# Opening of a two-block network: ten of sixteen modulation tiles made by TensorE as rows and turned, six left to VectorE

## The reference

```
mod_lat = silu(c) @ w_mod[0] + b_mod[0]        # 6 pieces of 1024: shift, scale, ...
mod_ctx = silu(c_ctx) @ w_mod[0] + b_mod[0]
u_ctx = h_ctx * (1 + mod_ctx[1]) + mod_ctx[0]  # 256 tokens
u_lat = h_lat * (1 + mod_lat[1]) + mod_lat[0]  # 512 tokens
lat = u @ mla_w_in                             # 1024 -> 512 + 256 + 64, then RMS norms
```

## Time and profile before

| | us |
|---|---|
| median of 3 runs (lowest, highest) | 4194.78 (4189.4, 4211.54) |
| the profiled execution, its own time | 4194.11 |
| its span, first to last instruction | 4192.3 |
| first matmul of the opening | 17.3 |
| first matmul behind the opening's barrier | 112.7 |
| mean granted TensorE clock | 0.967 of full speed |

### The profile page before, as it was taken

One profiled execution on the slowest core, in us unless ns is written; L12 is line 12 of the kernel. 1 busy time (PEld: TensorE's weight loads), 2 busy tenths in 40 slices (PEclk: granted clock), 3 DMA queues, 4 the chain that ended last, 5 costly groups with the idle time before them and its releaser, 6 DMA issues. The chain is left out here.

```text
span 4192.3 us, 53471 instructions
## 1 busy us (share of the span) xinstructions
PE 3870.7 (92%) x19878; PEld 2820.9 (67%) x19878; DVE 2551.6 (61%) x4594; ACT 1205.3 (29%) x2519; POOL 1304.3 (31%) x1515
## 2 busy tenths in 40 slices
PE   8899999999999797888999999989999989669998
PEld 4577555555555586777888886568755566668887
DVE  7634899652488884557688876645534428923354
ACT  3155310101222484652121112128611221341112
POOL 1175399200000068820000094849000111530001
PEclk9999999999999899999999999999999999879999
DMA  4542366331111076544345554523011375882222
GB/s 171 196 112 90 122 179 186 116 112 62 58 70 50 21 226 164 118 98 163 129 154 177 173 165 127 154 61 114 19 53 63 124 257 191 246 237 93 76 86 76
DMA packets 287968, 533.16 MB, mean 127 GB/s; under 512 B 177024, under 2 KB 184064, under 8 KB 263424
## 3 DMA queue, kind: packets, MB, share of 16 engines
q1 hardware_dynamic: 216736, 344.70, 25.5%
q0 software_dynamic: 53312, 180.00, 14.3%
q10 hardware_dynamic: 17696, 5.56, 0.6%
HBM read 430.01 MB, written 100.01 MB: 126 GB/s over the span
## 5 line engine op out<-in xcount | busy, mean ns | idle before, releaser
L570 PE MATMUL P<-hu,ring 128*128 128x384 f32 (+1 forms) x2448 | 743.0, 457 | 6.0 <-PEq L849 3.6
L570 PEld LDWEIGHTS P<-hu,ring 128*128 128x128 f32 x2448 | 465.5, 190 | 258.7 <-issue 5.8
L887 PE MATMUL P<-area,ring 128*128 128x256 f32 (+1 forms) x1880 | 484.4, 413 | 29.5 <-PEq L2605 16.0
L887 PEld LDWEIGHTS P<-area,ring 128*128 128x128 f32 x1880 | 356.1, 191 | 147.8 <-issue 38.4
L570 PE MATMUL P<-area,ring 128*128 128x256 f32 (+1 forms) x1584 | 443.2, 432 | 3.7 <-DVE area L733 3.0
L570 PEld LDWEIGHTS P<-area,ring 128*128 128x128 f32 x1584 | 301.7, 191 | 127.9 <-issue 5.4
L887 PE MATMUL P<-area,hu 128*128 128x256 f32 (+1 forms) x1104 | 297.2, 424 | 5.5 <-DVE hu L1010 5.5
L1147 POOL TENSOR_TENSOR fold<-mod,vec 128x16 f32<-128x16 f32 (+1 forms) x5 | 10.1, 2018 | 862.6 <-DMA s_fb<-area 365.0
L887 PEld LDWEIGHTS P<-area,hu 128*128 128x128 f32 x1104 | 209.3, 190 | 84.2 <-DVE hu L1010 7.7
L3010 DVE SCALAR_TENSOR_TENSOR area<-area 128x1024 f32<-128x1024 f32 x124 | 189.6, 1529 | 17.4 <-ACT area L3086 15.3
L2478 POOL TENSOR_TENSOR area<-area 128x512 f32<-128x512 f32 (+2 forms) x98 | 177.1, 1807 | 7.7
(11 more groups left out here) (495 smaller groups left out, 7193.4 us busy)
## 6 DMA issues: line engine op xcount, KB each, us to landing
ring<-in_w_ffn_in SPq DMA_DIRECT2D x44, 1024.0 KB, 4.8
area<-in_w_mod SPq DMA_DIRECT2D x70, 512.0 KB, 3.5
ring<-s_c POOLq DMA_DIRECT2D x18, 1152.0 KB, 9.4
stat<-in_w_mod SPq DMA_DIRECT2D x40, 512.0 KB, 3.4
s_c<-area POOLq DMA_DIRECT2D x32, 576.0 KB, 3.2
ring<-in_w_ffn_out SPq DMA_DIRECT2D x24, 704.0 KB, 4.1
area<-s_b POOLq DMA_DIRECT2D x16, 1024.0 KB, 6.0
hu<-s_c POOLq DMA_DIRECT2D x14, 1152.0 KB, 9.7
```

The source lines that it names most:

```text
L570: last = mm(to, col(a, k), b[:, k, :], start=fresh and k == 0, stop=k == q - 1, skip_group_check=True)
L887: last = mm(to, a[:, 128 * k:128 * k + 128], b[k], start=fresh and k == 0, stop=k == q - 1, skip_group_check=True)
```

## The change

Ten of the sixteen modulation tiles (0 to 7, 14 and 15) go from DVE to PE. Their weights are stored in another layout, two tiles together, so that PE can make a row of 256 outputs for both conditions: eight matmuls with a stationary operand of 128 x 2 (`silu_of[:, k, :]`, the silu of c and c_ctx as two columns) and 256 moving columns of weights, added up in two partitions of PSUM (`mod_row`). ACT copies the row to SBUF (`keep_row`), PE turns it back into columns with two matmuls of two moving columns (`turn_row`), and DVE adds the bias straight from PSUM. Five such pairs stand ahead of and between the products. The six tiles 8 to 13 stay on DVE.

The loads move: `conds` from the head of SP's queue to the head of POOL's, the first four projection weights as halves of 256 KB, those for k < 4 early on SP (`w_lo`), those for k >= 4 later on POOL (`w_hi`), `s5_lam` from SP to ACT. DVE makes six steps of the S5 tables between modulation tiles 1 and 2 and three more ahead of the last additions. The tails (256 tokens) of two output tiles share a PSUM bank, which frees one for the row; the copies of tiles 0 and 2 out of PSUM wait for the tile behind them, and tiles 1 and 3 are copied in two pieces.

```diff
+MOD_BY_PE = ((0, 8), (14, 16))
...
+    silu_of = c.view(25616, KD, 2)
+    row_kept = [c.view(24832 + 256 * n, 256)[0:2] for n in range(2)]
+    row = c.P[0:2, 1, 512:768]
+    pairs_of = [0, 2, 4, 6, 14]
...
-            sp.dma_start(flat(conds), ins["conds"][0:1, :].broadcast_to([128, 2 * D])).then_inc(conds_in, 16)
-            sp.dma_start(first_w[0], ins["w_mod"][0]).then_inc(mod_in[0], 16)
...
+            for k in range(0, KD, 2):
+                for n in (k, k + 1):
+                    sp.dma_start(first_w[n], ins["w_mod"][n]).then_inc(mod_in[n], 16)
                 sp.dma_start(h[:, k, 0:LAT], x[:, k, :]).then_inc(x_in[k], 16)
-            sp.dma_start(flat(raw), ins["s5_lam"]).then_inc(lam_in, 16)
+                if k == 0:
+                    for n in range(4):
+                        sp.dma_start(weights[n][:, 0:512], ins["w_mla_in"][n, :, 0:512]).then_inc(w_lo, 16)
+                sp.dma_start(h[:, k + 1, 0:LAT], x[:, k + 1, :]).then_inc(x_in[k + 1], 16)
...
+            pool.dma_start(flat(conds), ins["conds"][0:1, :].broadcast_to([128, 2 * D])).then_inc(conds_in, 16)
...
+            def mod_row(i):
+                n = pairs_of[i]
+                pe.wait_ge(mod_in[n], 16)
+                pe.wait_ge(mod_in[n + 1], 16)
+                if i == 0:
+                    pe.wait_ge(silu_v, 1)
+                else:
+                    pe.wait_ge(rows_kept, i)
+                for k in range(KD):
+                    last = mmul(row, silu_of[:, k, :], first_w[n + k // 4][:, 256 * (k % 4):256 * (k % 4) + 256],
+                                start=k == 0, stop=k == KD - 1, skip_group_check=True)
+                last.then_inc(rows_made, 1)
+            def turn_row(i):
+                if i == 0:
+                    pe.wait_ge(ident_in, 16)
+                pe.wait_ge(rows_kept, i + 1)
+                for e in range(2):
+                    last = mmul(turned_mod(pairs_of[i] + e), row_kept[i % 2][:, 128 * e:128 * e + 128], c.ident[0:2, 0:2],
+                                start=True, stop=True, skip_group_check=True)
+                last.then_inc(mods_turned, 1)
+            def product(k, between=()):
                 pe.wait_ge(shifted, k + 1)
+                if k == 0:
+                    pe.wait_ge(w_lo, 64)
+                if k == 4:
+                    pe.wait_ge(w_hi, 64)
                 for j in range(4):
-                    for a, b in BOTH:
-                        last = mmul(c.P[:, j, a:b], weights[j][:, 128 * k:128 * k + 128], u[:, k, a:b], start=k == 0, stop=k == KD - 1)
+                    w = weights[j][:, 128 * k:128 * k + 128]
+                    mmul(body(j), w, u[:, k, 0:512], start=k == 0, stop=k == KD - 1)
+                    last = mmul(tail(j), w, u[:, k, 512:T], start=k == 0 and j % 2 == 0, stop=k == KD - 1, skip_group_check=True)
                     if k == KD - 1:
                         last.then_inc(mm, 1)
+                    if j == 1:
+                        for i in between:
+                            turn_row(i)
+            mod_row(0)
+            turn_row(0)
+            product(0)
+            mod_row(1)
+            product(1, (1,))
+            product(2)
+            mod_row(2)
+            product(3, (2,))
+            product(4)
+            mod_row(3)
+            mod_row(4)
+            product(5, (3, 4))
+            product(6)
+            product(7)
...
+            act_fn(silu_of.rearrange("p k e -> p e k"), c.vec[:, at:at + 16].rearrange("p (e k) -> p e k", e=2), ACT.Silu).then_inc(silu_v, 1)
...
+            keep_row(0)
...
+            shift(0)
+            shift(1)
+            keep_row(1)
+            shift(2)
+            shift(3)
+            keep_row(2)
+            shift(4)
+            shift(5)
+            keep_row(3)
+            keep_row(4)
+            shift(6)
+            shift(7)
...
+            def scales(k):
+                dve.wait_ge(mod_in[8 + k], 16)
+                for cc in range(2):
+                    if k or cc:
+                        dve.wait_ge(made, 2 * k + cc)
+                    mod_product(c, 8 + k, cc, first_w[8 + k], junk).then_inc(made, 1)
+            def add(n, x):
+                return V.tensor_tensor(c.mod[:, n, 0:2], x, base[:, n:n + 1].broadcast_to([128, 2]), ALU.add)
+            def tile(k):
+                scales(k)
+                if k == 0:
+                    dve.wait_ge(based, 3)
+                dve.wait_ge(mods_turned, k // 2 + 1)
+                add(k, turned_mod(k))
+                dve.wait_ge(made, 2 * k + 2)
+                add(8 + k, c.mod[:, 8 + k, 0:2]).then_inc(added, 1)
+            dve.wait_ge(silu_c, 1)
+            tile(0)
+            tile(1)
```

More of the change, by code:

```diff
@@ L3139, in opening @@
     take = lambda *shape: (c.view(place[0], *shape), place.__setitem__(0, place[0] + int(np.prod(shape))))[0]
-    mag, ph, wrap, fs, fc = (take(K, N) for _ in range(5))
+    ph, wrap, mag, fs, fc = (take(K, N) for _ in range(5))
     pw = take(2, K, N)
@@ L3160, in opening @@
     mod_in, x_in, ctx_in = ([S(f"{w}{n}") for n in range(m)] for w, m in (("mod_in", 16), ("x_in", KD), ("ctx_in", KD)))
-    w_in = [S(f"w_in{n}") for n in range(7)]
+    w_in = [S(f"w_in{n}") for n in range(4, 7)]
+    w_lo, w_hi, silu_v, ident_in = S("w_lo"), S("w_hi"), S("silu_v"), S("ident_in")
+    rows_made, rows_kept, mods_turned = S("mod_rows"), S("mod_rows_kept"), S("mods_turned")
     made, added, shifted, mm, kept = (S(n) for n in ("mod_made", "mod_added", "shifted", "products", "lat_kept"))
@@ L3165, in opening @@
     c.s5_stored = stored = S("s5_stored")
-    pair = lambda k: c.mod[:, 0:16, 0:2].rearrange("p (a k) e -> p a k e", a=2)[:, :, k, :]
     with c.block() as block:
@@ L3205, in _ @@
             nc.gpsimd.tensor_scalar(base[:, 8:16], c.vec[:, 8:16], 1.0, None, ALU.add).then_inc(based, 1)
+            tile(2)
+            for n in range(4):
+                pool.dma_start(weights[n][:, 512:1024], ins["w_mla_in"][n, :, 512:1024]).then_inc(w_hi, 16)
+            for k in (3, 4, 5):
+                tile(k)
+            for n in (14, 15):
+                pool.dma_start(first_w[n], ins["w_mod"][n]).then_inc(mod_in[n], 16)
+            tile(6)
+            tile(7)
         @block.tensor
@@ L3220, in tile @@
             def tile(n, segs=BOTH):
-                pe.wait_ge(w_in[n], 16)
+                pe.wait_ge(w_in[n - 4], 16)
                 pe.wait_ge(kept, n - 3)
                 for a, b in segs:
+                    if a and n != 5:
+                        pe.wait_ge(kept, n - 2)
                     for k in range(KD):
@@ L3237, in _ @@
             tile(4)
-            pe.wait_ge(consts, 32)
+            pe.wait_ge(consts, 16)
             pe.wait_ge(kept, 4)
@@ L3258, in _, with keep_row, shift @@
             act.dma_start(c.vec[:, :], ins["vecs"]).then_inc(vecs_in, 16)
-            act.dma_start(c.ident[:, :], ins["ident"]).then_inc(consts, 16)
+            act.dma_start(c.ident[:, :], ins["ident"]).then_inc(ident_in, 16)
+            act.dma_start(flat(raw), ins["s5_lam"]).then_inc(lam_in, 16)
+            act.wait_ge(vecs_in, 16)
+            at = VEC_AT["c"]
+            act_fn(silu_of.rearrange("p k e -> p e k"), c.vec[:, at:at + 16].rearrange("p (e k) -> p e k", e=2), ACT.Silu).then_inc(silu_v, 1)
             act.wait_ge(conds_in, 16)
             act_fn(flat(conds), flat(conds), ACT.Silu).then_inc(silu_c, 1)
-            for k in range(KD):
+            def keep_row(i):
+                act.wait_ge(rows_made, i + 1)
+                if i >= 2:
+                    act.wait_ge(mods_turned, i - 1)
+                act_fn(row_kept[i % 2], row, ACT.Copy).then_inc(rows_kept, 1)
+            def shift(k):
                 act.wait_ge(added, k + 1)
@@ L3276, in keep @@
             def keep(n):
-                act.wait_ge(mm, n + 1)
-                act_fn(lat[:, n, :] if n < 6 else k_rope, c.P[:, n % 4, 0:T], ACT.Copy).then_inc(kept, 1)
+                act.wait_ge(mm, n + 2 if n in (0, 2) else n + 1)
+                to = lat[:, n, :] if n < 6 else k_rope
+                if n in (1, 3):
+                    act_fn(to[:, 0:512], body(n), ACT.Copy)
+                    act_fn(to[:, 512:T], tail(n), ACT.Copy).then_inc(kept, 1)
+                else:
+                    act_fn(to, c.P[:, n % 4, 0:T], ACT.Copy).then_inc(kept, 1)
             def square(n):
@@ L3314, in _ @@
         def _(dve):
[L3315 to L3329, removed]
             n = [0]
@@ L3345, in scaled, with tile @@
                 ins_.then_inc(unit, 1)
-            dve.wait_ge(added, KD)
+            def scales(k):
[6 more added lines that the diff above has]
+                return V.tensor_tensor(c.mod[:, n, 0:2], x, base[:, n:n + 1].broadcast_to([128, 2]), ALU.add)
+            def tile(k):
+                scales(k)
[6 more added lines that the diff above has]
+            dve.wait_ge(silu_c, 1)
+            tile(0)
+            tile(1)
             dve.wait_ge(ac, 1)
@@ L3353, in _ @@
```

(10 more changed lines are left out.)

19 lines of the change are left out of this document (5 added, 14 removed).

## The result

The changed kernel takes 4217.0 us (median of its runs), the kernel before 4195.88 in runs beside it: a ratio of 1.0049, 95% interval 1.0042 to 1.0056, thus 20.6 us more (17.6 to 23.5). The forecast was 4211, range 4195 to 4219.

A forecast was written before the change was run, and what follows sets the result against it. PE alone was taken to bound the opening: start 18.9, products 41.6, slow array 1.7, rows 14.0, turns 2.2, switches 1.7, wait 0.8 give 80.9 against 64.4. That is 16.5 later: 4194.8 + 16.5 = 4211.3 us, range 4195 to 4219.

The forecast's parts named there:

- start of product 0: PE's first product in the opening: starts at about 18.9 us, 1.6 later than before, after loads and DVE's products.
- eight products at full speed: PE in the opening: eight products of 3072 columns, 5.20 us each at full clock, 41.6 us together.
- slow array: PE in the opening: one fresh start at reduced speed costs 1.7 us, where before had two losses, 3.4.
- four rows: PE between products: four rows at 3.5 us each, the full price by moving columns, add 14.0 us.
- turns and switches: PE in the opening: four turns inside products cost 2.2 us, six pairs of stationary-shape switches 1.7.
- wait of row 4: PE in the opening: row 4 waits until ACT has copied row 3, 0.8 us with both hand-overs.
- end of the products: PE in the opening: the products end at 80.9 us against 64.4 before, 16.5 later.
- The bound: Opening: from 26.3 us PE alone sets its end; a microsecond there is one on the kernel, DVE's is worth nothing.
- Rivals 1 and 2: Opening: 1, narrow matmuls free beside wide ones, 4193.4 us, chance 0.07; 2, rows at a quarter price, 4200.5, chance 0.10.
- rival 3: Opening's loads: `conds` lands early on POOL, product 0 starts at 14.7, +12.3 us, 4207.1; chance 0.14.
- The forecast's own sign: Profile after, opening: the first product at 18 to 20 us, with ACT or DVE as its releaser.
- Rival 4: Opening starves: slow POOL loads, product 0 at 23.4 or later, array slow twice, over +21 us, 4217 to 4219; chance 0.15.

The follow-up runs named there:

- before with the longer stretch: The kernel before, with TensorE computing output tile 4 and the first sums of squares twice, nothing else changed: 4216.74 us, ratio 1.0046.

## Why the prediction was right, and where it was not

The terms of its sum, in us:

| term | predicted | measured |
|---|---|---|
| start of product 0 | 18.9 | 19.27 |
| eight products at full speed | 41.6 | 32 x 1.29 = 41.3 (24.41 to 25.70 is one output tile) |
| slow array | 1.7 | 7.82 - 5.36 = 2.5 |
| four rows | 14.0 | 4 x 3.54 = 14.2 |
| turns and switches | 3.9 | 3.4, what is left (0.60 + 0.60 + 1.05 are turns) |
| wait of row 4 | 0.8 | 0.56 |
| end of the products | 80.9 | 81.14 |

**The bound was right:** the opening is PE's chain, and the barrier moved by what the chain moved (16.9 and 16.9 us; 6.1 and 6.1 with whole rows). DVE's 18 us bought nothing, and the S5 tables stayed covered.

**Rows at full price: right.** Rivals 1 and 2 fell with it, by the timeline and by the doubled rows.

**Start of product 0: the number right, the step wrong.** The prediction had `conds` at 11.7, tile 8 at 14.2 and DVE's products as the last to end, and the half weights in by 14.5. `conds` landed at 1.3 + 8.9 = 10.2, tile 8 at 12.45, the shift ended at 16.5, as rival 3 had it in part; the half weights landed at 19.2 and set the start. The step that failed is taking SP's landing time for 2304 KB from before's rows, when the change had taken the load with the largest rows from SP and had cut its weights into rows of 2 KB. Of the 4.7 us by which the half weights came late, whole rows gave back 3.0. The other 1.7 go with what SP had moved by 10 us, 1.32 MB with halves and with whole rows against 1.72 in before, beside a POOL queue that now held `conds` and an ACT queue that held `s5_lam` (0.47 to 0.49 MB against 0.32); which of the two cost SP more was not tried. The chain over DVE ended 2.4 us earlier than forecast, the half weights 4.7 later, and the later of the two still fell near 18.9: that is luck. The forecast's own sign, ACT or DVE as the releaser of product 0, was not seen. Rival 4's mechanism, a start at 23.4 or later, did not occur, although the median fell at the time that it was priced at.

**The slow array was mis-sized.** The sum gave back 1.7 us because the profile of before shows two losses. Its second loss goes with a granted clock at half from 27.2 to 30.6 us, and the two other profiles of before have no such stretch: their seven products take 36.75 us, not 38.08. The first loss stands in all three, 1.7, 2.0 and 2.6 us over 5.20 (product 0 at 6.92, 7.21 and 7.79). The granted clock of 1.00 that the prediction reads there is no measurement: the traces of before have no clock record before 20.4, 21.2 and 21.6 us, and a stretch without a record reads 1.00. Product 0's loss is near half of the time from its start to that first record (1.5, 1.8 and 2.4). The changed kernel loses 2.5. Before loses 2.1 in product 0 in the mean of three, and 1.7 more in one of them, so next to nothing was given back.

**The 5.7 us between 4211.3 and 4217.0:** 0.4 is the opening's own error (16.9 for 16.5); 1.0 is the lateness of the one profile taken as the base; 1.1 is the median of before, 4195.88 over more runs. The remaining 3.2 lie behind the barrier, where the median leaves the changed kernel 4217.0 - 1.8 - 129.65 = 4085.5 us and before 4195.88 - 1.8 - 111.7 = 4082.4 (1.8 is what the own time has over the span). By the same sum before with the longer stretch has 4088.6, doubled rows 4086.3, all tiles on DVE 4084.6. Those 3 us are within the interval of the ratio; whether they are more than the scatter that goes with the clock stays open, and so do the 10 us of the version with pair 0 alone.

## What to carry to other kernels

Work moved onto the engine that bounds a stage costs its full length there, and the time that it saves on a waiting engine is worth nothing; a stationary operand of two columns brought no discount here. When loads are moved between queues, price the landing again from the bytes and the row sizes that then share the engines, not from where the same bytes stood before; and when a term is small, take the base from more than one profile.

## What the runs showed of the hardware

A pause of TensorE is paid after it ends: behind 5.3 us of waiting, product 0 with its way to row 1 took 7.82 us, at a granted clock of 0.50 until 24.29, and 5.36 at a clock of 1.00 once twelve small matmuls filled the pause.

Early in a profile a clock of 1.00 can mean that none is on record. The first line is the third profile of before, whose first clock record comes at 21.6 us: three records fill its 2 us. The second is the run with the filled pause, at a recorded 1.00: eight do.

```profile
17.00:19.00 2.00, 2.00 (x3) 0.92 (x4) 0.00 (x0) 0.00 (x0) 0.00 (x0) 1.00 1.02 400
20.00:22.00 2.00, 2.00 (x8) 1.25 (x7) 1.83 (x10) 1.31 (x2) 0.00 (x0) 1.00 1.03 389
```

While SP's and POOL's queues were both busy they had equally many packets (409 and 410, then 356 and 360), so their bytes went by the size of their rows. Halving the rows of a load, at the same bytes and place, delayed its landing by 3.0 us of 16.2.

A row of eight float32 matmuls with two stationary columns and 256 moving ones cost 3.46 us, by moving columns the price of 128 stationary columns.
